# Differential attention on one Trainium2 core: one wide bias tile per head, filled out by GpSimd, in place of three narrow bias operands per row

## What is computed

```python
MAX_DISTANCE, N_BUCKETS = 128, 32
bucket = _t5_bucket_2(kpos[None, :] - qpos[:, None])   # one bucket for every distance beyond the last step
bias = jnp.moveaxis(table[bucket], -1, 0)              # 4 heads
s = jnp.einsum('bqhmd,bkhmd->bmhqk', qblk, k) * scale + bias
p = jax.nn.softmax(s, axis=-1)
a = p[:, 0] - lam * p[:, 1]
o = jnp.einsum('bhqk,bkhd->bqhd', a, v)
```

## Time and profile before

| what | us |
|---|---|
| median of 3 executions | 3087.45 (3086.73 to 3089.76) |
| span of the profiled execution | 3083.0 |
| PE busy in it | 2962.9 |
| VectorE busy in it | 2024.5 |
| ScalarE busy | 1240.7 |
| GpSimd busy | 1609.1 |
| differential part of the attention stage | from about 2148 to 2329 |

### The profile page before, as it was taken

The page is one execution under the profiler, slowest core; times in us unless marked ns, Lnnn a source line. Parts: engine busy times, 40 slices in busy tenths (PEclk is TensorE's granted clock), DMA queues, the critical chain, the costliest instruction groups (busy, mean ns, idle before and its releaser), DMA issues.

```text
span 3083.0 us, 39500 instructions
## 1 busy us (share of the span) xinstructions
PE 2962.9 (96%) x12984; PEld 2316.6 (75%) x12984; DVE 2024.5 (66%) x2970; ACT 1240.7 (40%) x1988; POOL 1609.1 (52%) x1019
## 2 busy tenths in 40 slices
PE   8999998999999999999899999999999899999998
PEld 7788785668876778888787677578666688877886
DVE  7899965646254777777648632456984766675648
ACT  4321205630334544444222432355774466762221
POOL 3254333324441378888678334472002477777877
PEclk9999999999999999999999999999999999999999
DMA  3122410025110244444984122634322266789774
GB/s 125 36 89 100 148 53 14 1 80 208 54 69 21 103 151 163 163 163 166 339 301 171 51 85 107 190 97 102 101 66 92 86 259 259 264 308 348 264 256 178
DMA packets 156608, 449.30 MB, mean 146 GB/s; under 512 B 17085, under 2 KB 28517, under 8 KB 155721
## 3 DMA queue, kind: packets, MB, share of 16 engines
q1 hardware_dynamic: 128656, 369.68, 33.9%
q10 hardware_dynamic: 27832, 78.08, 6.8%
HBM read 298.25 MB, written 148.13 MB: 145 GB/s over the span
## 4 chain that ended last, share of the span: by engine, by line
PE 72%; DVE 8%; issue 8%; POOL 6%; ACT 3%; DMA 1%; SPq 0%; ACTq 0%; POOLq 0%; DVEq 0%
PE ps L1157 20%; PE ps L1159 19%; PE ps L1158 19%; POOL left_lo L850 4%; PE ps L1207 2%; PE ps L1400 2%; POOL part_in L845 2%; PE ps L1819 1%; PE ps L1807 1%; PE ps L1390 1%; PE ps L1792 1%; DVE sums_t L3292 1%; PE ps L1793 1%; DVE tmp L2877 1%; DMA part_in<-mlp_weights_dram 1%
## 5 line engine op out<-in xcount | busy, mean ns | idle before, releaser
L850 POOL TENSOR_TENSOR left_lo<-part_in,left_hi 128x512 fp32r<-128x512 f32 x414 | 576.2, 1406 | 247.1 <-ACT left_hi L2680 92.1
L739 POOL TENSOR_TENSOR w_hi<-w_raw,zero 128x1024 fp32r<-128x1024 f32 x70 | 135.0, 1929 | 490.9 <-PE ps L1159 486.3
L845 POOL TENSOR_TENSOR part_in<-part_in,part_in 128x512 f32<-128x512 f32 x252 | 361.1, 1433 | 40.7 <-DMA part_in<-mlp_weights_dram 19.3
L742 POOL TENSOR_TENSOR w_lo<-w_raw,w_hi 128x1024 fp32r<-128x1024 f32 x70 | 194.6, 2780 | 5.5
L1157 PE MATMUL ps<-h_hi,w_hi 128*128 128x512 f32 x480 | 188.3, 392 | 5.9 <-DVE h_lo L2871 5.9
L1158 PE MATMUL ps<-h_lo,w_hi 128*128 128x512 f32 x480 | 187.3, 390 | 0.0
L1159 PE MATMUL ps<-h_hi,w_lo 128*128 128x512 f32 x480 | 187.2, 390 | 0.0
L769 POOL TENSOR_TENSOR w_hi<-w_raw,zero 128x512 fp32r<-128x512 f32 x5 | 7.7, 1549 | 323.1 <-PE ps L1159 323.1
L1157 PE MATMUL ps<-down_t,left_hi 128*128 128x512 f32 x432 | 169.9, 393 | 6.7 <-DVE part_t L3197 2.6
L2964 DVE MATCH_REPLACE8 score<-top,score 128x1024 f32<-128x1024 f32 (+2 forms) x192 | 169.5, 905 | 0.0
L1158 PE MATMUL ps<-down_t,left_hi 128*128 128x512 f32 x432 | 168.9, 391 | 0.0
(11 more groups left out here) (605 smaller groups left out, 8728.0 us busy)
## 6 DMA issues: line engine op xcount, KB each, us to landing
w_raw<-weights_dram SPq DMA_DIRECT2D x102, 512.0 KB, 3.2
part_in<-ffn_weights_dram SPq DMA_DIRECT2D x144, 256.0 KB, 3.2
part_in<-mlp_weights_dram SPq DMA_DIRECT2D x144, 256.0 KB, 4.5
mlp_parts_scratch<-part_t SPq DMA_DIRECT2D x64, 512.0 KB, 4.5
down_t<-mlp_parts_scratch SPq DMA_DIRECT2D x64, 512.0 KB, 6.6
ffn_parts_scratch<-part_t SPq DMA_DIRECT2D x44, 512.0 KB, 4.4
down_t<-ffn_parts_scratch SPq DMA_DIRECT2D x44, 512.0 KB, 6.5
mlp_parts_scratch<-part_b SPq DMA_DIRECT2D x32, 512.0 KB, 4.9
```

The source lines that it names most:

```text
L739: nc.gpsimd.tensor_tensor(w_hi[s][:], raw[s][:], zero[:, 0:1].broadcast_to([P, 1024]), ALU.add).then_inc(w_rounded, 1)
L742: nc.gpsimd.tensor_tensor(w_lo[s][:], raw[s][:], w_hi[s][:].bitcast(F32), ALU.subtract).then_inc(w_split, 1)
L845: tt(part_in[p][dst][:], part_in[p][dst][:], part_in[p][other][:], ALU.add).then_inc(left_summed, 1)
L850: tt(lo[:], src[:], hi[:].bitcast(F32), ALU.subtract).then_inc(w_split, 1)
```

## The change

One tile `wide_bias` of 15 x 128 columns per slot takes the place of `e_bias`. SP loads the same 128 x 384 tile into its middle. GpSimd copies the leftmost of these columns over the 768 columns to the left, and the rightmost over the 768 to the right, before it goes on to the weight slabs of the next stage; these are 8 instructions, two for each head. For query tile i the 1024 columns that begin at (7 - i) x 128 are then the whole row of biases, so VectorE needs one instruction for each map. It writes minus (logits + bias) and takes the minimum, which is minus the maximum, so that the small reduction goes; the exponentials take scale -1. Each exponential waits for its own map only. VectorE waits at a head's first unit for the fills, no longer for the load.

```diff
-        e_bias = at("e_bias", late_at + 4 * KB, [P, 2, 3 * P])
+        wide_bias = at("wide_bias", BR + 36 * KB, [P, 2, 15 * P])
...
+        bias_widened, widened_0 = lam_exp, 1
...
-                sp.dma_start(e_bias[:, d % 2, :], t["bias_tiles_2"][d]).then_inc(bias_2_in[d % 2], 16)
+                sp.dma_start(wide_bias[:, d % 2, 6 * P:9 * P], t["bias_tiles_2"][d]).then_inc(bias_2_in[d % 2], 16)
...
-            pool.wait_ge(head_split, splits_before(MLA_HEADS))
+            for d in range(DIFF_HEADS):
+                tile = wide_bias[:, d % 2, :]
+                pool.wait_ge(bias_2_in[d % 2], 16 * (d // 2) + 16)
+                for wing, far in ((slice(0, 6 * P), 6 * P), (slice(9 * P, 15 * P), 9 * P - 1)):
+                    nc.gpsimd.tensor_tensor(tile[:, wing], tile[:, far:far + 1].broadcast_to([P, 6 * P]),
+                                            zero[:, 0:1].broadcast_to([P, 6 * P]), ALU.add).then_inc(bias_widened, 1)
...
-                act.wait_ge(a_max, unit + 1)
                 if d < 0:
+                    act.wait_ge(a_max, unit + 1)
...
                 for m, row in enumerate((prob_rows[g][q], second[unit % 2])):
-                    nc.scalar.activation(row[:], row[:], ACT.Exp, bias=e_stat[:, unit % 8, 3, m:m + 1],
+                    act.wait_ge(e_red, 2 * d + m + 1)
+                    nc.scalar.activation(row[:], row[:], ACT.Exp, bias=e_stat[:, unit % 8, 3, m:m + 1], scale=-1.0,
                                          accum_out=e_stat[:, unit % 8, 4, m:m + 1]).then_inc(a_exp, 1)
...
-                i, bias = unit % NT, e_bias[:, d // NT % 2, :]
+                i, first = unit % NT, (NT - 1 - unit % NT) * P
                 if i == 0:
-                    dve.wait_ge(bias_2_in[d // NT % 2], 16 * (d // NT // 2) + 16)
-                near0, near1 = max(0, i - 1) * P, min(NT, i + 2) * P
-                b0 = P if i == 0 else 0
+                    dve.wait_ge(bias_widened, 2 * (d // NT) + widened_0 + 2)
...
                     dve.wait_ge(a_qk, NT * MLA_HEADS + 2 * d + m + 1)
-                    for kind, lo, hi, b in ((0, 0, near0, bias[:, 0:1].broadcast_to([P, near0])),
-                                            (2, near1, S, bias[:, 3 * P - 1:3 * P].broadcast_to([P, S - near1])),
-                                            (1, near0, near1, bias[:, b0:b0 + near1 - near0])):
-                        if lo < hi:
-                            ins = nc.vector.tensor_tensor_reduce(row[:, lo:hi], wide(m)[:, lo:hi], b, 1.0, TAKEN,
-                                                                 ALU.add, ALU.max, stats[:, kind, m:m + 1])
-                    ins.then_inc(e_red, 1)
-                dve.wait_ge(e_red, 2 * d + 2)
-                kinds = slice(0 if near0 else 1, 3 if near1 < S else 2)
-                nc.vector.tensor_reduce(stats[:, 3, :], stats[:, kinds, :].rearrange("p k m -> p m k"), AX.X, ALU.max,
-                                        negate=True).then_inc(a_max, 1)
+                    nc.vector.tensor_tensor_reduce(row[:], wide(m), wide_bias[:, d // NT % 2, first:first + S], -1.0, -TAKEN,
+                                                   ALU.add, ALU.min, stats[:, 3, m:m + 1]).then_inc(e_red, 1)
```

## The result

| | before | after |
|---|---|---|
| median, same chip | 3088.14 us (3080.85 to 3091.43, 14 runs) | 3092.51 us (3087.96 to 3097.07, 14 runs) |
| span of the profiled execution | 3083.0 | 3086.2 |
| from the first transposes of group 7 to those of group 15 | 161.43 | 165.03 |

The ratio is 1.0016, with a 95% interval of 1.0009 to 1.0023: some 4.4 us slower, where 2.25 us less were forecast. 3092.5 lies above the range (3081.3 to 3089.2). In size it is still under the 0.2% that I set as "no change", but the interval leaves out 1.

What follows compares the result with a forecast made beforehand. PE was taken to set the pace inside groups, waiting for VectorE at group starts and in group 7. Terms -1.0 - 1.65 + 0.4 = -2.25 us took 3087.45 to 3085.2, range 3081.3 to 3089.2.

Steps and rivals of the forecast that it cites:

- The fills: GpSimd's idle time: eight fills of 1.47 us and the slabs behind them finish before their readers; all covered.
- The very next paragraph: VectorE beside GpSimd: fills cost 0.4 us, bounds nothing to 8.8; at 896.94 a 1.22 us instruction took 2.07 beside a copy.
- The wide instruction: VectorE's instruction over 1024 columns takes 1.22 us, with bounds 0.953 and 1.285.
- Group 7 and the starts: PE's waits for VectorE: 1.0 us saved in group 7, 1.65 us at the starts of groups 8 to 14.
- The waits at starts: At group starts, PE's 0.5 us wait before transposes stays; waits for slots 0 and 1 fall to 0.2 to 0.4.
- The fills on VectorE: Differences beside GpSimd's fills: 0.4 us lost in all, from head 1; heads 2 and 3 covered by slack.
- nearly gone: Sign expected in group 7: PE's first wait for VectorE almost disappears.
- Slack inside groups: Inside groups VectorE needs 4.16 us a unit instead of 4.66, under PE's 4.44; late work saved is worth nothing.
- the first: Rival: differences just after a bias lands are held by fills, up to 2.9 us per head 1 to 3; 3093.6; chance 0.10.
- The clock rival: PE's clock in the last group: its fall to 0.50 goes (3083.3) or a second comes (3087.1); chance 0.12 together.
- a second fall comes: Case of the clock rival: PE's clock falls once more after waits, giving 3087.1 us.
- The reference time: Whole kernel before the change: executions' median 3087.45 us, 4.45 above the profiled span of 3083.0.

Runs made afterwards that it cites:

- e10: The changed kernel itself, run again unedited as a base: 3092.07 us, ratio 1.0011 to the kernel before.
- e1: Against the changed kernel: the two weight slabs are split before the four bias fills instead of after; 3085.28 us, ratio 0.9995 to the kernel before.
- e7: The kernel of e1 run again unedited as a base: 3084.28 us, ratio 0.9994 to the kernel before.
- e2: Against the kernel before: GpSimd waits for head 3's bias load before splitting the slabs; no fills, no wide instruction; 3090.47 us, ratio 1.0006.
- e5: Against e1: behind the last fill GpSimd adds an idle 128x768 tile to itself five times, reading SBUF; 3086.60 us, ratio 0.9997 to the kernel before.
- e9: Against the changed kernel: the slabs, still behind the fills, wait for unit 52's maxima, just after a group start; 3084.48 us, ratio 0.9990 to before.

## Why the prediction was wrong

**The step that failed** is the last of "The fills": "The slabs behind the last fill, two of some 4.5 us, would be split by about 2256; PE needs them after 2329 ... All covered". The time of day was right (they end at 2254.9). Priced was whether the slabs come in time for their readers. Not priced was what they do while they run. The very next paragraph priced that for the fills, with the row at 896.94 as evidence, and its upper bound counted "6 fills of 1.47 = 8.8 us". The four slab instructions read SBUF as the fills do, are longer (1.89 and 2.40 us at 2098 in the kernel before), and were moved beside the differences by the same edit. Priced like the fills they stand for up to 8.6 us (twice 1.89 and twice 2.40). Measured: 7.30 us of VectorE, 4.92 of them on PE's path, and 1.45 more by the clock (0.87 in e10). It is the mechanism that was left out there, not a size: the sum had no term for the slabs.

Point by point:

- **The wide instruction**: forecast 1.22, measured 1.216 and 1.220. Right.
- **Group 7 and the starts**, -1.0 and -1.65, together -2.65: the stage of e1, where the slabs' cost is absent, is 2.71 shorter. Group 7 gave 1.01 (21.71 to 20.70 us): VectorE's stretch without a pause, 2160.47 to 2173.62, is 2159.97 to 2172.12 in the changed kernel. The seven groups behind it gave 1.70, and by turns as forecast: groups 8, 10, 12 and 14 are 0.31 to 0.33 us shorter in e1 than before, groups 9, 11 and 13 are 0.14 shorter, where 0.30 and 0.15 were forecast. Right in both parts, and in the mechanism.
- **The waits at starts**: the one before the transposes stayed at 0.34 in the rows, as forecast. Those for slots 0 and 1 came down to 0.35 and 0.21 us, worked out as in the prediction from the starts 2211.67, 2212.81 and 2213.95; forecast were 0.2 to 0.4. Group 7's waits for slots, 0.67 and 1.09 before and 0.51 and 0.75 after, shrank far less than "nearly gone".
- **The fills on VectorE**, +0.4: measured zero on the path. Head 1's fills in group 7, 2160.51 to 2163.40, ended just before the difference's first instruction at 2163.66, a miss by 0.3 us that the prediction did not foresee. Head 2's took 1.66 us of VectorE, all covered by the wait of 2.27. In e7's trace heads 2 and 3 lost 2.04 and 2.14 us, and both groups still lasted 19.72. The cover is this wait, not the 0.28 us a unit that I had named.
- **Slack inside groups**: "What late work it no longer has is worth nothing" holds, but it had a use I did not give it: the wait before the last difference, at the place of the slabs, is 2.27 us after and 1.22 before, and what is lost just ahead of it is taken up by it. By this the faster VectorE softened the slabs' cost by some 1.05 us, an estimate from the two waits.
- **The rivals**: the first had the right mechanism, the wrong GpSimd instructions, and the right size only by luck (3093.6). The clock rival had "a second fall comes", +1.9; it came, through this wait, and cost 0.87 to 1.45 us. The fall in the last group, its other case, comes and goes by itself: the changed kernel's trace has it and e10's has not, and it costs 1.70 us (14.25 us from the transposes to `finish` against 12.55), not 1.9.
- **The reference time**: 3087.45 was the median of three executions; the 14 beside the change gave 3088.14. That is 0.7 us of the 7.3 by which the forecast was off. The rest, 6.6, is the slabs as far as the spread allows to say: the change and e1 are 6.3 us apart in the stage (e10 and e7 5.8) and 6.5 in their medians' distance to before (7.5).

The version with the slabs in front of the fills is better than the changed kernel in every comparison here, by 5.8 to 6.3 us in the stage. Against the kernel before its stage is 2.7 us shorter, and its medians 2.2 and 3.9 lower, while the intervals of both ratios just reach 1: a gain seen in the traces, and too small for this many executions to prove in the time.

## What to carry to other kernels

When an edit adds work to an engine's queue, list what stands behind it and price each piece twice at its new place: is it still in time for its reader, and whom does it disturb while it runs. A GpSimd instruction that reads SBUF costs VectorE up to its whole length for each VectorE instruction with two SBUF operands that it meets, however small that one is; so put such GpSimd work beside VectorE work that reads PSUM. What reaches the path depends on what VectorE does next. Straight ahead of one of its own waits, only the loss beyond that wait got through (2.38 of 7.30 us and 2.39 of 3.70 were absorbed by a wait of 2.27, 1.31 of 4.63 in e2 by one of 1.22); behind the wait all of it did (1.49, e5). Further ahead 0.98 of 2.75 us got through although the wait was 2.27 (e9), for PE needed a slot from VectorE before that wait was reached. So find the next point at which the other engine needs VectorE, and how much idle time lies before it.

## What the runs showed of the hardware that was not expected

- A VectorE instruction of 128x1 with two SBUF operands is held as long as a large one: 1.72 and 1.66 us in place of 0.22. It is the first of a pair, and while it waits the engine gains nothing: as soon as it is through, GpSimd's next instruction starts, and the large one waits again.
- GpSimd is held as well: 2.87 in place of 1.89 us behind a difference (2249.60), and in e9 3.25 in place of 2.40.
- The clock's answer to a wait of PE varies. After 5.26 us it was 0.50 and then 0.71 in two stretches of 4 us, after 5.28 in e10 0.70 and 0.88, and the next group was 1.45 and 0.87 us too long. In the last group all traces have the same waits of PE, 1.67 and 0.25 to 0.34 us. Yet two executions of one kernel, e1 and e7, differ there: four products take 3.58 us in the one and 1.96 in the other, and the group 14.17 and 12.55.

```profile
2311.85 3.58 PE L1826 MATMUL ps<-pt_plain,v_plain 128*128 128x512 f32 x4 [0.34 <-ACT pt_plain L2595]
```

```profile
2311.86 1.96 PE L1826 MATMUL ps<-pt_plain,v_plain 128*128 128x512 f32 x4 [0.34 <-ACT pt_plain L2595]
```

Of the 13 traces 7 are long there (14.17 to 14.25 us) and 6 short (12.55). What decides between the two was not tried, and stays open; a single trace's last group is no evidence for or against a change.
